# Decoder layer on one core: order of VectorE's work on V in the first five groups, PSUM banks of the last 64 dense tokens, first weight slot in pieces

## What is computed

```python
def block(xb):                                   # PEER, per block of tokens
    q = einsum('td,de->te', xb, w_q)             # 8 heads, two halves of 128
    s = einsum('thcd,hckd->thck', q, sub_keys)
    ...                                          # best 16 of 128 in each half, best 16 of their sums
    gw = softmax(top_v)
    u, v = exp_u[eidx], exp_v[eidx]              # 128 experts per token
    a = gelu(einsum('td,thkd->thk', xb, u))
    return einsum('thk,thkd->td', gw * a, v)
```

## Time and profile before

| | |
|---|---|
| median of 3 runs | 2060.76 us (2059.99 to 2066.89) |
| the profiled execution | 2066.74 us, span 2065.0 us |
| TensorE (PE) | 1975.2 us busy, 96% of the span |
| VectorE (DVE) | 1267.6 us, 61% |
| ScalarE (ACT) | 641.5 us, 31% |
| GpSimd (POOL) | 176.8 us, 9% |
| mean granted clock of TensorE | 0.971 |
| moved by DMA | 548.31 MB, mean 266 GB/s |

### The profile page before, as it was taken

The page is one execution under the profiler, slowest core; times in us unless marked ns, Lnnn a source line. Parts: engine busy times, 40 slices in busy tenths (PEclk is TensorE's granted clock), DMA queues, the critical chain, the costliest instruction groups (busy, mean ns, idle before and its releaser), DMA issues.

```text
span 2065.0 us, 27408 instructions
## 1 busy us (share of the span) xinstructions
PE 1975.2 (96%) x11300; PEld 1772.4 (86%) x11300; DVE 1267.6 (61%) x1851; ACT 641.5 (31%) x828; POOL 176.8 (9%) x216
## 2 busy tenths in 40 slices
PE   7999999999889999998889999999999999999996
PEld 7998998889679999997666779899899898898894
DVE  5434454566563696875666565665765765765756
ACT  4333455344333102323434222232222222222321
POOL 1000122000000000010000111111111111111100
PEclk9889999999889999999999999999999999999998
DMA  7454432756234675886888898998998998988961
GB/s 288 163 177 166 168 123 103 285 184 225 104 140 157 231 266 197 293 303 222 276 269 271 332 383 301 358 378 342 363 366 341 382 350 341 395 341 339 402 255 41
DMA packets 124106, 548.31 MB, mean 266 GB/s; under 512 B 57952, under 2 KB 58016, under 8 KB 59600
## 3 DMA queue, kind: packets, MB, share of 16 engines
q1 hardware_dynamic: 52496, 374.36, 47.5%
q0 software_dynamic: 20096, 147.04, 18.8%
q10 hardware_dynamic: 51392, 25.17, 4.6%
HBM read 530.74 MB, written 14.68 MB: 264 GB/s over the span
## 4 chain that ended last, share of the span: by engine, by line
PE 85%; issue 5%; DVE 5%; ACT 4%; DMA 1%; POOL 0%; SPq 0%; ACTq 0%; DVEq 0%
PE bank L838 22%; PE bank L521 16%; PE bank L765 10%; PE bank L536 10%; PE bank L796 4%; PE bank L799 4%; PE bank L795 4%; PE bank L797 4%; PE bank L798 4%; ACT split_a L1104 2%; PE bank L785 2%; DVE rows L1509 2%; ACT split_b L1104 1%; PE bank L561 1%; DVE wt L1553 1%
## 5 line engine op out<-in xcount | busy, mean ns | idle before, releaser
L1168 DVE TENSOR_TENSOR ring_lo<-ring_raw,ring_hi 128x2048 fp32r<-128x2048 f32 x97 | 222.2, 2291 | 216.4 <-ACT ring_hi L876 216.2
L521 PE MATMUL bank<-actT_hi,ring_hi 128*128 128x256 f32 x912 | 264.6, 290 | 14.4 <-DVE ring_lo L1168 12.1
L521 PE MATMUL bank<-actT_lo,ring_hi 128*128 128x256 f32 x912 | 262.0, 287 | 0.0
L521 PE MATMUL bank<-actT_hi,ring_lo 128*128 128x256 f32 x912 | 261.8, 287 | 0.0
L838 PEld LDWEIGHTS bank<-h2T,experts 128*128 128x128 f32 x1408 | 229.4, 190 | 1.5
L838 PE MATMUL bank<-h2T,experts 128*128 128x192 f32 x1408 | 230.6, 326 | 0.0
L838 PE MATMUL bank<-h2T,late_raw 128*128 128x192 f32 x1408 | 230.6, 326 | 0.0
L838 PEld LDWEIGHTS bank<-h2T,late_raw 128*128 128x128 f32 x1408 | 229.1, 190 | 0.0
L876 ACT CAST ring_hi<-ring_raw 128x2048 fp32r<-128x2048 f32 x97 | 184.9, 1906 | 104.4 <-PE bank L536 91.6
L765 PE MATMUL bank<-h2T,experts 128*128 128x192 f32 x1280 | 216.3, 326 | 0.0
L765 PEld LDWEIGHTS bank<-h2T,experts 128*128 128x128 f32 x1280 | 206.9, 190 | 0.0
(11 more groups left out here) (243 smaller groups left out, 3269.0 us busy)
## 6 DMA issues: line engine op xcount, KB each, us to landing
experts<-in_stream SPq DMA_DIRECT2D x168, 1024.0 KB, 6.5
ring_raw<-in_stream SPq DMA_DIRECT2D x97, 1024.0 KB, 4.8
late_raw<-in_stream SPq DMA_DIRECT2D x88, 1024.0 KB, 8.8
gate_matrix<-stage ACTq DMA_DIRECT2D x12, 1024.0 KB, 4.8
gbuf<-gate_matrix ACTq DMA_DIRECT2D x32, 384.0 KB, 9.6
gb<-in_ln_g POOLq DMA_DIRECT2D x3, 1024.0 KB, 6.8
gb<-in_ln_b POOLq DMA_DIRECT2D x3, 1024.0 KB, 9.7
act_raw<-in_xT SPq DMA_DIRECT2D x4, 512.0 KB, 9.2
```

The costliest lines, as they stand in the source:

```text
L521: last = pe.matmul(bank[n % 2][:, 0:T], ring[w][:, s % R, k * P:(k + 1) * P], act[x][:, k, :], start=(k == 0 and i == 0), stop=(k == KO - ...
L1168: dve.tensor_tensor(ring_lo[:, r, :], ring_raw[:, r, :], ring_hi[:, r, :].bitcast(F32), ALU.subtract).then_inc(lo_ready, 1)
```

## The change

Three edits.

1. V stage: `v_low(c)` stands between `gated(c)` and `w_low(c)`; before, `v_low(c + 1)` stood behind `w_low(c)`.
2. Banks: tokens 128 to 191 accumulate in banks 4 to 7, one per quarter, from the first V chunk to the last late group, without an evacuation; tokens 0 to 127 use four banks in the V stage and two in turn in the late groups. The additions into `accC` and the four copies at the end of the V stage are gone; ScalarE copies the four banks in the last group, one behind each quarter. `folded` uses banks 0 and 1 and takes `hrow` first.
3. Start: slot 0 is loaded and split in four pieces of 512 columns, each behind the quarter of x that goes with it; slots 1 to 3 follow whole.

```diff
-            for s in range(R):
-                k = slice(4 * s, 4 * s + 4)
-                sp.dma_start(act_raw[:, k, :], a["xT"][:, k, :]).then_inc(x_landed[s], 16)
+            for q in range(4):
+                k, c = slice(4 * q, 4 * q + 4), slice(512 * q, 512 * q + 512)
+                sp.dma_start(act_raw[:, k, :], a["xT"][:, k, :]).then_inc(x_landed[q], 16)
+                sp.dma_start(ring_raw[:, 0, c], a["stream"][0][:, c]).then_inc(first_landed[q], 16)
+            for s in range(1, R):
                 sp.dma_start(ring_raw[:, s, :], a["stream"][s]).then_inc(landed[s], 16)
...
+                    if s == 0 and k % 4 == 0:
+                        if k < 12:
+                            pe.wait_ge(first_lo, k // 4 + 1)
+                        else:
+                            pe.wait_ge(lo_ready, 1)
...
+            def split_products(c, hi, lo, whole, j, first, final, fresh=False):
+
+                rest = bank[C_BANK + j]
+                pe.matmul(whole[:, :], w_split[:, c, 0:P], hi, start=first, stop=False, skip_group_check=True)
+                pe.matmul(whole[:, :], w_split[:, c, 2 * P:3 * P], hi, start=False, stop=False, skip_group_check=True)
+                pe.matmul(rest[:, :], w_split[:, c, P:2 * P], hi, start=fresh, stop=False, skip_group_check=True)
...
-                pe.wait_ge(v_out, 4 + 2 * (NQ * (LATE_G - 1) + j + 1))
+                pe.wait_ge(c_out, j + 1)
                 if j >= 2:
                     pe.wait_ge(dve_nb, 16 + j - 1)
                 cols = slice(j * 512, (j + 1) * 512)
-                pe.matmul(bank[6 + j % 2][:, :], fold[:, 0:P], accC[:, cols], start=True, stop=False)
-                pe.matmul(bank[6 + j % 2][:, :], fold[:, NS:NS + P], hrow[:, cols], start=False, stop=True).then_inc(back_ready, 1)
+                pe.matmul(bank[j % 2][:, :], fold[:, NS:NS + P], hrow[:, cols], start=True, stop=False)
+                pe.matmul(bank[j % 2][:, :], fold[:, 0:P], accC[:, cols], start=False, stop=True).then_inc(back_ready, 1)
...
-                    pe.wait_ge(v_out, 4 + max(0, 2 * (NQ * g + j - 1)))
+                    pe.wait_ge(v_out, 4 + max(0, NQ * g + j - 1))
...
-            for n, j in enumerate(V0_LAST):
-                if n < NQ - 1:
-                    act.wait_ge(v_bank, n + 1)
-                else:
-                    act.wait_ge(v_used, N_EARLY)
-                act.copy(accC[:, j * 512:(j + 1) * 512], bank[V0_BANKS[j][1]][:, :]).then_inc(c_out, 1)
-
...
+                    if g == GROUPS_P - 1 and i % 2:
+                        act.wait_ge(v_used, 8 * g + i + 1)
+                        act.copy(accC[:, i // 2 * 512:(i // 2 + 1) * 512], bank[C_BANK + i // 2][:, :]).then_inc(c_out, 1)
...
-                dve.tensor_tensor(hres[:, 0, cols], hres[:, 0, cols], bank[outs[0]][:, :], ALU.add).then_inc(v_out, 1)
-                dve.tensor_tensor(accC[:, cols], accC[:, cols], bank[outs[1]][:, :], ALU.add).then_inc(v_out, 1)
+                dve.wait_ge(v_out, 4 + max(0, NQ * (g - EARLY_G - 1) + j + 1))
+                dve.tensor_tensor(hres[:, 0, cols], hres[:, 0, cols], bank[2 + j % 2][:, :], ALU.add).then_inc(v_out, 1)
...
-            v_low(2)
             for c in range(2):
                 w_low(c)
             for m in range(N_EARLY):
...
                     gated(early_chunk(c), c)
+                    v_low(c)
                     w_low(c)
-                if RH <= c + 1 < N_EARLY:
-                    v_low(c + 1)
                 gathers(IN_G + IN_LOADING + IN_V0 * (m + 1) // N_EARLY)
...
-            dve.wait_ge(c_out, NQ)
...
-V0_BANKS = ((2, 3), (4, 5), (6, 7), (0, 1))
+V0_BANKS = (2, 3, 0, 1)
 V0_FIRST = (0, 1, 2, 3)
-V0_LAST = (3, 0, 1, 2)
+V0_LAST = (3, 2, 0, 1)
+C_BANK = 4
```

More of the change, by code:

```diff
@@ L279, in build @@
         landed = [sem(f"landed{r}") for r in range(R)]
+        first_landed = [sem(f"first_landed{q}") for q in range(3)] + [landed[0]]
+        first_hi = sem("first_hi")
+        first_lo = sem("first_lo")
         hi_ready = sem("hi_ready")
@@ L511, in block_slot @@
             def block_slot(s, n, lap=None, fresh=None, tiles=(0, KO)):
-                if tiles[0] == 0:
+                if tiles[0] == 0 and s:
                     pe.wait_ge(lo_ready, s + 1 if lap is None else lap + (s + 1))
@@ L790, in _ @@
                 early_slot(k)
-            def split_products(c, hi, lo, banks, first, final):
-                both, small = banks
-                pe.matmul(both[:, :], w_split[:, c, 0:P], hi, start=first, stop=False, skip_group_check=True)
-                pe.matmul(both[:, :], w_split[:, c, 2 * P:3 * P], hi, start=False, stop=False, skip_group_check=True)
-                pe.matmul(small[:, :], w_split[:, c, P:2 * P], hi, start=first, stop=False, skip_group_check=True)
-                pe.matmul(both[:, :], w_split[:, c, 0:P], lo, start=False, stop=final, skip_group_check=True)
-                return pe.matmul(small[0:ND - P, :], w_split[:, c, P:ND], lo, start=False, stop=final, skip_group_check=True)
+            def split_products(c, hi, lo, whole, j, first, final, fresh=False):
[3 more added lines that the diff above has]
+                pe.matmul(rest[:, :], w_split[:, c, P:2 * P], hi, start=fresh, stop=False, skip_group_check=True)
+                pe.matmul(whole[:, :], w_split[:, c, 0:P], lo, start=False, stop=final, skip_group_check=True)
+                return pe.matmul(rest[0:ND - P, :], w_split[:, c, P:ND], lo, start=False, stop=final, skip_group_check=True)
             pe.wait_ge(idx_out, 2)
@@ L807, in _ @@
                 for j in V0_LAST if final else V0_FIRST:
-                    if c == 0 and j == 1:
+                    if c == 0 and j == 0:
                         pe.wait_ge(g_out, QUADS)
-                    if c == 0 and j == 3:
+                    if c == 0 and j == 2:
                         pe.wait_ge(tb_out, N_U + N_EARLY)
                     cols = slice(j * 512, (j + 1) * 512)
-                    last = split_products(c % 8, hi[:, cols], lo[:, cols], [bank[b] for b in V0_BANKS[j]], c == 0, final)
+                    last = split_products(c % 8, hi[:, cols], lo[:, cols], bank[V0_BANKS[j]], j, c == 0, final, c == 0)
                     if final and j != V0_LAST[-1]:
@@ L830, in _ @@
                     tile, landing, count = raw_slot(2 * N_EARLY + PER_G * g + i)
-                    if c == N_EARLY:
-                        pe.wait_ge(v_out, 1)
-                        pe.wait_ge(c_out, 1)
-                    else:
+                    if c < N_EARLY + 2:
+                        pe.wait_ge(v_out, 1 + i)
+                    if c > N_EARLY:
                         pe.wait_ge(tb_out, N_U + c - 1)
@@ L853, in _ @@
                             cols = slice(c4 * 512, (c4 + 1) * 512)
-                            last = split_products(c, hi[:, cols], lo[:, cols], pair(j), c == 0, c == 7)
+                            last = split_products(c, hi[:, cols], lo[:, cols], bank[2 + j % 2], j, c == 0, c == 7)
                         last.then_inc(v_used, 1)
@@ L858, in _ @@
                             pe.wait_ge(row_used, 2 * GATHERS)
+                            pe.wait_ge(tb_out, N_U + 8 * GROUPS_P)
                         folded(j - 1)
@@ L899, in _ @@
                 act.copy(actT_hi[:, q, :], act_raw[:, q, :]).then_inc(act_hi, 1)
-                if k < AHEAD:
-                    high(k)
+                c = slice(512 * k, 512 * k + 512)
+                act.wait_ge(first_landed[k], 16)
+                act.copy(ring_hi[:, 0, c], ring_raw[:, 0, c]).then_inc(first_hi if k < 3 else hi_ready, 1)
+            for s in range(1, AHEAD):
+                high(s)
             for n in range(8):
@@ L1178, in _ @@
                 part((actT_hi[:, q, :], actT_lo[:, q, :]), act_raw[:, q, :]).then_inc(act_lo, 1)
-                if k < AHEAD:
-                    low(k)
+                c = slice(512 * k, 512 * k + 512)
+                if k < 3:
+                    dve.wait_ge(first_hi, k + 1)
+                else:
+                    dve.wait_ge(hi_ready, 1)
+                part((ring_hi[:, 0, c], ring_lo[:, 0, c]), ring_raw[:, 0, c]).then_inc(first_lo if k < 3 else lo_ready, 1)
+            for s in range(1, AHEAD):
+                low(s)
             dve.wait_ge(act_lo, A_X)
```

11 lines of the change are left out of this document (3 added, 8 removed).

## The result

The changed kernel takes **2010.33 us**, the median of four runs (2008.37 to 2012.31); the kernel before 2062.15 us (four runs, the three of the table and one more, 2059.99 to 2066.89). The ratio is 0.9753, with a 95% interval of 0.9724 to 0.9783. The profiled execution took 2009.67 us, its span is 2007.8 us at a mean granted clock of 0.979.

What follows compares the result with a forecast made beforehand. The V stage was taken as bound by a loop of ScalarE casts and VectorE remainders, not TensorE. Savings of 40.7 + 8.2 + 4.5 = 53.4 us from 2066.74 give 2013.3, or 2007.4 off the median; forecast 2011, range 2003 to 2023.

Steps and rivals of the forecast that it cites:

- The loop of casts: V stage: ScalarE's cast and VectorE's remainder wait on each other, 4.79 us a chunk; cutting it saves 40.7 us.
- together 4.1 us: V stage: VectorE's own work per chunk, 3.22 us plus 0.92 for gathers, against TensorE's 4.61 us.
- First late group, 8.2 us less: First late group: the gate load is issued earlier, ending VectorE's 14.21 us wait; 8.2 of 8.5 lost us return.
- one small piece a turn: First late group: the gate load gets one piece per 8 KB packet of other loads; stall wholly gone, 0.3 us more.
- Start, 4.5 us less (2 to 5): Kernel start: TensorE begins near 8 us and slot 1 at 19.1; 4.5 us less, bounds 2 and 5.0.
- Banks and tail, 0: Late groups and end: dropping 44 VectorE additions and moving four ScalarE copies changes the time by 0.
- sum of 53.4 us: Whole kernel: V stage 40.7, first late group 8.2 and start 4.5 us less, taken from the profiled 2066.74 us.
- the choice of 2011 between 2013.3 and 2007.4: Whole kernel: 2013.3 if the profiled run's 6 us above the median belong to the stall, 2007.4 if not; 2011 taken.
- The ends of the range: Whole kernel: low 2003 with all bounds good, high 2023 with the gate load late and the start at its lower bound.
- Rival A: First late group: the gate load is late as before and the group keeps its 87 us; 2021.5 us, chance 0.12.
- Rivals B and C: V stage: B, V slots land late, 2043 us, chance 0.08; C, gate loads starve, 2220 us, chance 0.05.
- a sign of being wrong: V stage: the forecast would be wrong if gate loads in it take over 20 us.

Runs made afterwards that it cites:

- the second trace: The unmodified changed kernel profiled again, its span 2000.4 us; the five runs of that repeat have a median of 2006.68 us, ratio 0.9729 to the kernel before.
- the four loads held back: On the kernel before, SP issues the first late group's four 1 MB loads only once the V stage's last gate load has landed: 2044.35 us, ratio 0.9915.
- the two pairs with equal half clock: U products' end: kernel before 939.51 us, with only edit 3 added 936.43; kernel before with only edit 1 added 937.73, changed kernel without edit 1 934.60.
- the whole remainder twice: On the changed kernel, VectorE computes each remainder of V in the V stage two times with the same result: 2057.39 us, one run.

## Why the prediction was right

The forecast was 2011 us in a range of 2003 to 2023; measured were 2010.33. By its steps:

- **The loop of casts is cut and TensorE becomes the bound.** Shown: the chain is made of V products, and undoing the order alone brings the loop back. The term was 40.7 us; from 230.46 to 188.25 it is 42.2. 4.59 us a chunk held (4.61 forecast). Of the difference, 0.9 us is the first chunk, which lost 1.6 us to half clock in place of 2.5 (in the second trace nothing), and 0.7 the other 39 chunks.
- **VectorE's work per chunk, "together 4.1 us", was mis-sized.** It added the lengths of rows, which overlap. The step from start to start gives 3.7 with the gather's share, and the windows had it all along: 151.33 us busy in the earlier trace rows over 40 chunks is 3.8. The slack is 0.9 to 1.1 us, not 0.5. It didn't show in the time, since TensorE is the bound with either.
- **First late group, 8.2 us less.** Measured 8.5. The forecast let the gate load keep its 45.1 us and land 32 us into the group; it took 8.7 and landed before the group began. That its time stayed at 45.1 was the part that was mis-sized, by a factor of five, at a price of 0.3 us. The Trainium skill, "DMA: Bandwidth & Descriptors", "Queues, rings and completion order", says that a DMA engine goes round its queues packet by packet; a packet is a group of descriptors there, so the forecast's one small piece a turn is not what it states. The counts above, 280 against 281, do come out as one for one, though they don't show single turns. The times fit in direction: 6.3 us with the four loads held back, 8.7 with a lead of 4.3 us, 27.8 with 0.4, 45.1 with 0.1. The lead alone doesn't fix the time, since the order alone had 4.4 us of it and took 24.1 until the last few packets had landed.
- **Start, 4.5 us less (2 to 5).** At slot 1's first matmul it is 4.74 (24.36 to 19.62). Slot 1 landed at 15.35 where 14.8 was forecast, but the kernel before began it at 24.36 and not at the 24.1 of the forecast, so of two errors of 0.5 and 0.3 us only the difference shows (5.0 by its working). What reaches the V stage is 3.1 us, as the two pairs with equal half clock show: the term was too large by 1.4, within its bounds. The forecast named the reason, a slow half-clock start of slot 1, at up to 1.5 us, and took 0.5 off for it. With the start alone, slot 1 takes 7.34 us (20.02 to 27.36), against 5.90 in the kernel before, whose first half clock lies from 21.3 to 24.7 us, ahead of slot 1's work for the most part.
- **Banks and tail, 0.** Shown for the banks (ratio 0.9982, interval with 1 in it) and by the 808.2 us that all traces have from the second late group to the end.
- **The basis, and luck.** The sum of 53.4 us stood against 57.2 in the spans: the V stage gave 1.5 more than its term and the late group 0.3, the start 1.4 less, and 3.4 us ahead of the V stage are half of the 6.8 us by which the changed kernel's trace was shorter at half clock (68.3 us against 75.1), in code that the change does not touch. That the median is within 0.7 us of the forecast is partly luck, since these cancel against the choice of 2011 between 2013.3 and 2007.4. That choice was a guess, and its reason (part of the 6 us might be the stall) isn't borne out: the runs of before spread over 15 us in one batch, and all four traces with the old order and the loads not held back have the stall, with 85.6 to 87.8 us. The ends of the range are added up wrongly by about a us: by the forecast's own terms they are 2004.4 and 2024.0, and the result lies inside these too.
- **Rival A**, the gate load late as before: fell. With its lead taken away it takes 27.8 us, and the group still loses nothing. The limit of about 358 GB/s for a core that the Trainium skill names, "DMA: Bandwidth & Descriptors", "Bandwidth", would have brought this case, as the forecast put it. The same section gives this figure as what each of two cores gets when both stream from their part of HBM, and here one core runs; the late group's window shows 401 GB/s over 78.49 us.
- **Rivals B and C**, V slots or gate loads late inside the V stage: fell. DMA moved 326 GB/s (318 forecast) and TensorE waited for no slot. But one gate load inside the V stage, issued at 979.92 us, took 20.8 us, which is over the 20 that the forecast had named as a sign of being wrong; the others took 3.6 to 13.1. It stayed below the 22 us ahead of its use, and nothing waited for it.

## What to carry to other kernels

Where two engines each wait for the other a good part of a stage, read the chain of waits: if it never touches the busiest engine, the order of one engine's own program may be the bound, and moving one instruction behind work whose inputs are a step older cost nothing here. Take an engine's work per step from the starts of its rows, or from its busy time over the number of steps, not from the sum of lengths. A small load that somebody will need soon should be issued a few microseconds ahead of the large ones: its time went from 45 us to 9 here, or to 24 where a few of its packets were left behind.

## What was not expected of the hardware

**The spread of the runs goes with TensorE's half clock, mostly ahead of the V stage.** The kernel before spreads from 2052.5 to 2068 us over 17 runs of one batch, its shortest run at a mean granted clock of 0.981 and its longest at 0.971. Every trace takes 808.2 us from the second late group on. Kernels whose code is the same up to the V stage reach its first V product at different times: before at 944.42 us, the one with the 1 MB loads held back at 931.14. A stretch that shows it, in the windows of before and then of that kernel:

```profile
515.00:550.00 35.00, 29.21 (x131) 23.13 (x131) 12.45 (x27) 13.20 (x29) 0.00 (x0) 0.76 0.24 85
```

```profile
515.00:550.00 35.00, 29.22 (x127) 22.99 (x126) 20.47 (x37) 15.68 (x30) 0.00 (x0) 0.95 0.27 92
```

TensorE is busy and idle by turns in both, about 29.2 of 35 us, but the granted clock is 0.76 in one and 0.95 in the other; in the second the work behind is further on (VectorE 20.47 us against 12.45). Ahead of the V stage the clock was at half (1.2 GHz) for 75.1 us in the trace of before, 71.7 with the order alone, 64.9 with the banks alone and 44.4 with the loads held back. Half of each difference, 1.7, 5.1 and 15.4 us, is what half clock costs where TensorE works all the time; the U products ended 1.8, 4.8 and 13.3 us earlier. In the changed kernel's second trace half clock was 17.1 us shorter than in its first, and they ended 5.9 us earlier. So 13.3 us of what the kernel with the loads held back won lie ahead of the V stage. Whether holding the loads back has anything to do with it is open: they are issued later in the program than these stretches, but none of its four runs took longer than 2051.63 us. An effect of a few microseconds is therefore read in this kernel from the stage it acts in, not from the medians.

**DMA moved more than 400 GB/s over a whole late group**: 401 in the changed kernel, 409 with the loads held back.

**GpSimd's indirect DMAs look longer with the new order.** Its busy time in the V stage rose from 16.4 to 45.9 us for the same 16 instructions. It isn't the speed of the stage: with the whole remainder twice, a stage of 232.7 us has 44.8, and with a quarter of it twice, one of 184.6 us has 23.5. The traces don't show why; no wait of the stage is put down to them.
